# Products of ones placed on TensorE behind four norms' spreads and in the router

## The chip, the cores and the metric

The kernel runs on one core of a Trainium2 chip. The time is the device time of one execution in microseconds (us), taken as the median of several runs. One further execution is recorded by the hardware profiler, and all rows below are from it. [...]

## The reference, cut to what matters

The program computes two transformer blocks one after the other for 256 tokens of width 1024. The first has two layers, and in its layer 0 a context of 256 more tokens goes along. Each layer normalises, modulates, projects, mixes (attention and a long convolution), and then does the same with a gated feed-forward part:

```python
h = modulate(rms_norm(x, norm_mix[layer]), shift1, scale1)
q, k, v, hy, g = jnp.split(h @ w_in[layer], PROJ_SPLITS, axis=-1)
...
x = x + gate1 * x_mix
x = x + gate2 * swiglu(modulate(rms_norm(x, norm_ffn[layer]), shift2, scale2),
                       w_gate_up[layer], w_down[layer])
```

The second block has a mixer, a cross attention to a memory, and a mixture of 32 experts of which each token uses two. A router picks them: logits, a group, the two best experts of it, their gates, and the place of each token in its expert's list.

## The kernel before, in words

Activations lie with their features on the 128 partitions and tokens along the row: 512 columns (tokens and context) in layer 0, 256 in layer 1 and later. Weights come in units of 512 KB through a ring of six slots on SyncE's queue. ScalarE rounds a unit to its high part (`ac_split`, L434) and VectorE subtracts for the low part (`ve_split`, L442). Each product of a weight tile then is three matmuls, high by high, high by low and low by high (`pe_block`, L463; `pe_pair`, L478, does two blocks side by side, key by key).

A norm goes over all engines. ScalarE squares, VectorE adds the squares of tiles 0 to 6 (`ve_add_square`, L532), TensorE sums over the partitions with a column of ones (`pe_sum_seven`, L516, and `pe_sum_last`, L523), ScalarE takes the root (L559), VectorE the reciprocal (L570), and TensorE spreads the result to all partitions by `pe_spread` (L539): one product of 128 columns for each 128 tokens, in plain fp32. The trace shows each such fp32 product as two instructions, so a spread of four is a row of x8. Then the normalised tile k is made in a chain of four steps: VectorE multiplies by the root (L854), ScalarE scales and shifts (L835), GpSimd or ScalarE copies the high part (L847, L840), VectorE subtracts for the low part (L862). TensorE's next work, `pe_pair`, needs tile 0 to begin with (`pe.wait_ge(*ve_norm.at("low", ...))`) and a further tile after every six matmuls.

Four norms are followed by such a pair: "mix0" (before layer 0), "ffn0" (its feed-forward part, spread at the end of `pe_mix_out(0)`), "mix1" (at the end of `pe_down(0)`) and "ffn1" (at the end of `pe_mix_out(1)`). At "mix0" the spread comes early and two groups of modulation products (L601, L617) stand between it and the pair.

The order of the work on each engine is written out by hand in one program per engine (`tensor_program`, `scalar_program` and so on). PSUM banks are handed out in turn from a list: `banks.take` moves the first idle bank to the end of the list, and whoever takes a bank waits for its last reader.

In the router (`pe_router_steps`) TensorE transposes the logits and 16 tiles of the activations (`pe_to_rows`, L2262), then waits for VectorE's selection (`chosen`, L2337) and multiplies it by a triangle for the places (L2249 to L2254). The gather of the tokens (L2382) and the experts' products (L2433, L2477) follow. The experts' weights, 192 units of 1 MB, come on SyncE's queue (L2868) through 15 slots; the first 15 are queued behind the last weights of the cross attention, and every further one waits until its slot is spent.

Of the kernel before, what the change touches and what calls it, by code (L numbers as in the profile page):

```python
# [16 lines left out]
P = 128  # L17
# [253 lines left out]
def two_blocks_kernel(nc, T):  # L271
    ctx = ExitStack()
    with ctx:
        def sb(name, cols, dt=F32, rows=P):
            return ctx.enter_context(nc.sbuf_tensor(name, [rows, cols], dt))
# [31 lines left out]
        ones = sb("ones", P)  # L307
# [83 lines left out]
        banks = Slots([b[:, :] for b in psum])  # L391
# [143 lines left out]
        def pe_spread(pe, site, cols, give=True):  # L535
            pe.wait_ge(*landed["con"])
            pe.wait_ge(*ve_norm.at("rstd", site))
            for tb in range(cols // P):
                ins = pe.eng.matmul(banks.ap("sum", site)[:, tb * P:(tb + 1) * P],  # L539
                                    rsts.ap(site)[:, tb:tb + 1].to_broadcast([P, P]), ident, start=True, stop=True)  # L540
            ins.then_inc(*pe_sums.up("spread", site))
            if give:
                banks.give("sum", site)

        def ac_square(ac, site, n, chunk, cols):
            ac.wait_ge(*squares.emptied(site, n))
# [44 lines left out]
        def pe_mod_group(pe, g):  # L591
            if g == 0:
                banks.hold((ve_mod, ("added", 0, 0)), "mods")
            out = banks.take((ac_mod, ("rows", g)), "mod", g)
            pe.wait_ge(*banks.emptied("mod", g))
            pe.wait_ge(*ve_mod.at("silu", 1))
            for k in range(8):
                w, u = first.block("w_mod", 0, 32 * g + 4 * k, 4)
                pe.wait_ge(*first.arrived(u))
                c = k % 4  # L600
                ins = pe.eng.matmul(out[32 * c:32 * c + 32, :], sc2[:, k, :], w, start=k < 4, stop=k >= 4,  # L601
                                    tile_position=(0, 32 * c))
            ins.then_inc(*pe_mod.up("group", g))
            if g > 0:
                pe_mod_turn(pe, g - 1)
            if g == 3:
                pe_mod_turn(pe, g)
                banks.give("mods")
# [260 lines left out]
        def tokens(l):  # L869
            return 256 if l else 512  # L870
# [552 lines left out]
        def pe_mix_out(pe, l):  # L1423
            t, site = tokens(l), f"ffn{l}"

            def q_cut(k):
                pe.wait_ge(*ve_cut.at("q", l, k))

            pe_open(pe, site)
            pe_added(site)  # L1430
            for j in range(8):
                out = banks.take((ve_out, ("mix", l, j, t // 256 - 1)), "mix", l, j)
                pe.wait_ge(*banks.emptied("mix", l, j))
                pe_block(pe, ("mix", l, j), out[:, 0:t], "w_out", l, 8 * j, 8, lambda k: (hi_q(k, l), QL[:, k, 0:t]), q_cut)
            pe_sum_seven(pe, site, t)
            pe_sum_last(pe, site, t)
            pe_spread(pe, site, t)

        def ac_mix_out(ac, l):
            t, site = tokens(l), f"ffn{l}"  # L1440
# [137 lines left out]
        def pe_down(pe, l):  # L1578
            t, site = tokens(l), down_site(l)
            pe_added(site)  # L1580

            def three(half, k, n):
                m, b = 22 * half + k, 88 * half + 4 * k + n
                u, c = unit("w_down", l, b), (b % UB) * P
                hi, lo = cut_place(VTR, m, t), cut_place(YFR, m, t)
                pe.wait_ge(*ve_cut.at("ff", l, m))
                pe.wait_ge(*ve_lo.at(nth[u]))
                whi, wlo = hi_slot(nth[u])[:, c:c + P], lo_slot(u)[:, c:c + P]
                for i, (w, x) in enumerate(((whi, hi), (whi, lo), (wlo, hi))):
                    ins = pe.eng.matmul(banks.ap("ff", l, 4 * half + n)[:, 0:t], w, x, start=k == 0 and i == 0, stop=k == 21 and i == 2)  # L1590
                return ins, u

            for half in range(2):
                for n in range(4):
                    banks.hold((ve_out, ("ff", l, 4 * half + n, t // 256 - 1)), "ff", l, 4 * half + n)
                for n in range(4):
                    pe.wait_ge(*banks.emptied("ff", l, 4 * half + n))
                for k in range(19 if half else 22):
                    for n in range(4):
                        ins, u = three(half, k, n)  # L1600
                        if k == 21 and n < 3:
                            ins.then_inc(*pe_products.up("ff", l, half, n))
                    ins.then_inc(*pe_products.up("down", l, half, k))
                    stream.spent[u] = (pe_products, ("down", l, half, k))
                if half:
                    for n in range(4):
                        for k in range(19, 22):
                            ins, u = three(half, k, n)
                            stream.spent[u] = (pe_products, ("down", l, 1, 21))
                        ins.then_inc(*pe_products.up("ff", l, half, n) if n < 3 else pe_products.up("down", l, 1, 21))  # L1610
                for n in range(4):
                    banks.give("ff", l, 4 * half + n)
            if l == 0:
                pe_open(pe, site)
                pe_sum_seven(pe, site, t)
                pe_sum_last(pe, site, t)
                pe_spread(pe, site, t)


        def ac_down_squares(ac, l, j):  # L1620
# [615 lines left out]
        def pe_router_steps(pe):  # L2236
            out = banks.take((ve_router, ("logits", 1)), "by_token")
            pe.wait_ge(*banks.emptied("by_token"))
            pe.wait_ge(*ac_router.at("logits"))
            for tb in range(2):  # L2240
                ins = pe.eng.transpose(out[:, 36 * tb:36 * tb + 36], LT[:, tb * P:(tb + 1) * P], ident[0:36, 0:36])
            ins.then_inc(*pe_router.up("by_token"))
            pe_to_rows(pe, 0)
            pe_to_rows(pe, 1)
            out = banks.take((ve_router, ("place",)), "place")
            pe.wait_ge(*banks.emptied("place"))
            pe.wait_ge(*ve_router.at("chosen"))
            tri, both = LATE[:, 2, :], MM.rearrange("p b e -> p (b e)")
            pe.eng.matmul(out[:, 0:64], tri, both, start=True, stop=False)  # L2249
            pe.eng.matmul(out[:, 32:64], ones[:, :], MM[:, 0, :], start=False, stop=True).then_inc(*pe_router.up("place"))  # L2250
            out = banks.take((ve_router, ("most",)), "total")
            pe.wait_ge(*banks.emptied("total"))
            pe.eng.matmul(out[:, 0:32], ones[:, :], MM[:, 0, :], start=True, stop=False)
            pe.eng.matmul(out[:, 0:32], ones[:, :], MM[:, 1, :], start=False, stop=True).then_inc(*pe_router.up("total"))  # L2254

        def pe_to_rows(pe, tb):
            for half in range(2):
                out = banks.take((ac_router, ("rows", tb, half)), "rows2", tb, half)
                pe.wait_ge(*banks.emptied("rows2", tb, half))
                for k in range(4):  # L2260
                    pe.wait_ge(*ac_router.at("gain", 4 * half + k))
                    ins = pe.eng.transpose(out[:, k * P:(k + 1) * P], H2[:, 4 * half + k, tb * P:(tb + 1) * P], ident)  # L2262
                ins.then_inc(*pe_router.up("rows", tb, half))
# [444 lines left out]
        def tensor_program(pe):  # L2708
            pe_mod_group(pe, 0)
            pe_mod_group(pe, 1)  # L2710
            pe_open(pe, "mix0")
            pe_added("mix0")
            pe.wait_ge(*gp_start.at("ones"))
            pe_sum_seven(pe, "mix0", 512)
            pe_sum_last(pe, "mix0", 512)
            pe_spread(pe, "mix0", 512)
            pe_mod_group(pe, 2)
            pe_mod_group(pe, 3)
            for l in range(2):
                pe_heads(pe, l)  # L2720
                pe_hyena(pe, l)
                for n, a in enumerate(attention(l)):
                    pe_attend(pe, a, no_side if n else convolving(l, pe_conv_step))
                pe_merge(pe, l)
                pe_mix_out(pe, l)
                pe_gate_up(pe, l)
                pe_down(pe, l)
            pe_keys(pe)
            pe_mixer(pe)
            pe_mixed(pe)  # L2730
            pe_memory(pe)
            pe_router_steps(pe)
            pe_moe(pe)
            pe_output(pe)
# [274 lines left out]
```

## Time and profile before

| | |
|---|---|
| median of 3 runs | 2119.44 us (2115.68 to 2121.33) |
| profiled execution | 2115.06 us, of which the span of the instructions is 2113.3 us |
| TensorE busy | 1905.0 us (90%), 14008 matmuls |
| VectorE, ScalarE busy | 1133.7 us (54%), 891.7 us (42%) |
| granted TensorE clock, mean | 0.957 |
| DMA | 427.99 MB, mean 203 GB/s |

"Span" is the time from the first to the last instruction; the profiled execution's own time is 1.8 us longer. A busy time is the sum of the intervals in which an engine worked. In rows of the timeline the last bracket is the time for which the engine idled before that instruction, and who ended it. Matmuls are pipelined: a row's second number for x16 is from the start of the first to the end of the last, and the step from one to the next is shorter than one's own duration.

### The profile page before, as it was taken

How to read it: one execution, taken by the hardware profiler on the slowest of the kernel's cores; microseconds unless marked ns; L12 is line 12 of the kernel's file. 1: busy time of each engine (PE TensorE's matmuls, PEld its weight loads, DVE VectorE, ACT ScalarE, POOL GpSimd, SP SyncE). 2: the span in 40 equal slices, each digit the busy share in tenths (PEclk: the TensorE clock that was granted, in tenths of full speed). 3: DMA queues.
4: the chain of work that ended last, by engine and by line, in shares of the span. 5: the costliest groups of instructions: out<-in, count | busy, mean ns of one | idle time of the engine just before them, and what ended most of it. 6: DMA issues, size and time to landing. Idle time of an engine off the chain costs nothing.

```text
span 2113.3 us, 33439 instructions
## 1 busy us (share of the span) xinstructions
PE 1905.0 (90%) x14008; PEld 1544.2 (73%) x14008; DVE 1133.7 (54%) x1862; ACT 891.7 (42%) x1514; POOL 16.9 (1%) x31
## 2 busy tenths in 40 slices
PE   7999989999999999999899999999999777677766
PEld 3877667777777888788699999997898544455434
DVE  3454756666787788557655667779765111111011
ACT  4333445554766667444444555744845100000001
POOL 0000000000000000000000000000000000000000
PEclk9999999999999999999999999999999988888897
DMA  7222014453555555224045455543247999999995
GB/s 311 87 70 80 1 61 148 150 189 109 181 179 180 190 192 174 100 80 160 1 159 194 160 184 185 189 161 119 80 160 290 419 420 420 419 419 420 420 420 217
DMA packets 91120, 427.99 MB, mean 203 GB/s; under 512 B 11089, under 2 KB 12754, under 8 KB 66002
## 3 DMA queue, kind: packets, MB, share of 16 engines
q1 hardware_dynamic: 78866, 382.51, 48.3%
q10 hardware_dynamic: 12096, 43.26, 6.1%
q8 instruction: 113, 1.85, 0.4%
q14 instruction: 45, 0.37, 0.0%
HBM read 424.68 MB, written 1.05 MB: 201 GB/s over the span
## 4 chain that ended last, share of the span: by engine, by line
PE 67%; DMA 19%; DVE 7%; ACT 4%; issue 2%; SPq 1%; POOL 0%; DVEq 0%; ACTq 0%; POOLq 0%
PE bank L463 43%; PE bank L1590 8%; DMA area<-in_w 7%; DMA his<-in_w 4%; DMA ring<-in_w 4%; DMA PPT<-in_w 2%; PE bank L478 2%; PE bank L2477 2%; PE bank L2433 2%; DVE st L1261 1%; PE bank L1189 1%; PE bank L2085 1%; ACT PPT L1206 1%; PE bank L928 1%; DVE ring_r L442 1%
## 5 line engine op out<-in xcount | busy, mean ns | idle before, releaser
L463 PE MATMUL bank<-HH_r,his_r 128*128 128x256 f32 (+1 forms) x1504 | 501.9, 334 | 1.3 <-DVE ring_r L442 1.2
L442 DVE TENSOR_TENSOR ring_r<-ring,his_r 128x1024 fp32r<-128x1024 f32 x306 | 373.7, 1223 | 223.3 <-ACT his_r L434 222.0
L463 PE MATMUL bank<-HH_r,ring_r 128*128 128x256 f32 (+1 forms) x1504 | 490.3, 326 | 0.0
L463 PE MATMUL bank<-H_r,his_r 128*128 128x256 f32 (+1 forms) x1440 | 472.3, 328 | 0.0
L434 ACT ACTIVATE his_r<-ring 128x1024 fp32r<-128x1024 f32 x306 | 322.6, 1056 | 321.5 <-PE bank L463 233.9
L463 PEld LDWEIGHTS bank<-HH_r,his_r 128*128 128x128 f32 x1504 | 282.4, 188 | 36.9 <-issue 10.0
L463 PEld LDWEIGHTS bank<-HH_r,ring_r 128*128 128x128 f32 x1504 | 282.1, 188 | 24.8
L463 PEld LDWEIGHTS bank<-H_r,his_r 128*128 128x128 f32 x1440 | 270.5, 188 | 28.7 <-issue 2.6
L2449 DVE TENSOR_TENSOR tmp<-tmp,bank 128x128 f32<-128x128 f32 x64 | 18.4, 288 | 384.4 <-ACT tmp L2442 264.2
L2433 PE MATMUL bank<-area,KF 128*32 128x128 f32 x1888 | 87.6, 311 | 39.9 <-DMA area<-in_w 36.8
L463 PE MATMUL bank<-area_r,his_r 128*128 128x256 f32 (+1 forms) x384 | 121.9, 317 | 0.0
L1590 PE MATMUL bank<-VT_r,ring_r 128*128 128x512 f32 (+1 forms) x352 | 118.6, 337 | 0.0
L1590 PE MATMUL bank<-YF_r,his_r 128*128 128x512 f32 (+1 forms) x352 | 118.1, 335 | 0.0
L1590 PE MATMUL bank<-VT_r,his_r 128*128 128x512 f32 (+1 forms) x352 | 117.5, 334 | 0.0
L2433 PEld LDWEIGHTS bank<-area,KF 128*32 128x32 f32 x1888 | 70.9, 125 | 54.0 <-DMA area<-in_w 46.8
L2488 ACT ACTIVATE H<-bank 128x512 f32<-128x512 f32 x16 | 9.6, 597 | 195.5 <-PE bank L2477 195.5
L703 ACT ACTIVATE rst<-rst 128x1024 f32<-128x1024 f32 x80 | 83.5, 1044 | 0.6 <-DVE rst L695 0.6
L2477 PE MATMUL bank<-area,tmp 128*32 128x512 f32 x256 | 60.7, 680 | 22.4 <-DMA area<-in_w 21.7
L463 PEld LDWEIGHTS bank<-area_r,his_r 128*128 128x128 f32 x384 | 72.1, 188 | 5.8 <-issue 0.2
L1590 PEld LDWEIGHTS bank<-YF_r,his_r 128*128 128x128 f32 x352 | 66.1, 188 | 7.7
L1590 PEld LDWEIGHTS bank<-VT_r,his_r 128*128 128x128 f32 x352 | 65.9, 187 | 7.6 <-DVE YF_r L1333 0.2
L1329 ACT ACTIVATE VT_r<-area 128x512 fp32r<-128x512 f32 (+1 forms) x96 | 50.0, 524 | 50.9 <-PE bank L1590 45.3
(408 smaller groups left out, 3327.3 us busy)
## 6 DMA issues: line engine op xcount, KB each, us to landing
area<-in_w SPq DMA_DIRECT2D x91, 1024.0 KB, 27.2
ring<-in_w_in SPq DMA_DIRECT2D x102, 512.0 KB, 3.5
ring<-in_w_gate_up SPq DMA_DIRECT2D x88, 512.0 KB, 3.6
ring<-in_w SPq DMA_DIRECT2D x36, 1024.0 KB, 27.2
HH<-in_w SPq DMA_DIRECT2D x26, 1024.0 KB, 26.9
ring<-in_w_down SPq DMA_DIRECT2D x44, 512.0 KB, 3.5
KX<-in_w_mod_rows ACTq DMA_DIRECT2D x28, 512.0 KB, 3.4
VX<-in_w_mod_rows ACTq DMA_DIRECT2D x28, 512.0 KB, 3.5
```

The costliest lines, as they stand in the source:

```text
L434: ac.eng.activation(hi_slot(n), stream.slot(u), ACT.Copy).then_inc(*ac_hi.up(n))
L442: ve.eng.tensor_tensor(lo_slot(u), stream.slot(u), hi_slot(n).bitcast(F32), ALU.subtract).then_inc(*ve_lo.up(n))
L463: ins = pe.eng.matmul(out, a, b, start=k == 0 and m == 0, stop=end)
L478: ins = pe.eng.matmul(out, a, b, start=k + m == 0, stop=k == 7 and m == 2)
L703: ac.eng.activation(prod, prod, ACT.Copy, accum_out=MODS[l][:, j, s:s + 1]).then_inc(*ac_mod.up("sum", n, s))
L928: ins = pe.eng.matmul(vb[tb // 2][:, o:o + 256], x[:, k, sl], w, start=k == 0 and n == 0 and o == 0, stop=k == 7 and n == 2 and o > 0)
L1189: ins = pe.eng.matmul(out[:, 0:256], vs(kc), c.pts[g % 2][:, kc * 256:(kc + 1) * 256], start=kc == 0, stop=kc == c.nk - 1)
L1206: ac.eng.activation(p[:, m * w:(m + 1) * w], src[:, m * w:(m + 1) * w], ACT.Exp, bias=st[:, so + m:so + m + 1], scale=c.rq(h, i + m) if c. ...
L1329: ac.eng.activation(hi, src, ACT.Copy).then_inc(*ac_cut.up(*key))
L1590: ins = pe.eng.matmul(banks.ap("ff", l, 4 * half + n)[:, 0:t], w, x, start=k == 0 and i == 0, stop=k == 21 and i == 2)
L2433: ins = pe.eng.matmul(out[32 * n:32 * n + 32, 0:P], HG[g % 2][:, k, 32 * j:32 * j + 32], w, start=k == 0, stop=k == 7, tile_position=(0, 3 ...
L2477: ins = pe.eng.matmul(out[32 * j:32 * j + 32, :], AT[j][:, 32 * k:32 * k + 32], w, start=k == 0, stop=k == 3, tile_position=(0, 32 * j))
```

## The change

A helper `pe_idle` is added. It takes a bank, waits until it is free and until `ones` is set (which was at the very start), and issues n products of `ones` (128x128) by `ones` into the bank's first 128 columns, each overwriting the last. Nothing reads the bank. It is called with n = 12 between the modulation products and the first pair, 14 behind the spread of ffn0, 14 behind that of mix1, 10 behind that of ffn1, and 9 in the router between the transposes and the places.

```diff
--- before.py
+++ after.py
@@ -542,6 +542,15 @@
             if give:
                 banks.give("sum", site)
 
+
+        def pe_idle(pe, site, n):
+            out = banks.take((pe_sums, ("idle", site)), "idle", site)
+            pe.wait_ge(*banks.emptied("idle", site))
+            pe.wait_ge(*gp_start.at("ones"))
+            for i in range(n):
+                ins = pe.eng.matmul(out[:, 0:P], ones[:, :], ones[:, :], start=True, stop=True)
+            ins.then_inc(*pe_sums.up("idle", site))
+
         def ac_square(ac, site, n, chunk, cols):
             ac.wait_ge(*squares.emptied(site, n))
             ac.eng.activation(squares.ap(site, n)[:, 0:cols], chunk, ACT.Square).then_inc(*ac_squares.up(site, n))
@@ -1435,6 +1444,7 @@
             pe_sum_seven(pe, site, t)
             pe_sum_last(pe, site, t)
             pe_spread(pe, site, t)
+            pe_idle(pe, site, 14 if l == 0 else 10)
 
         def ac_mix_out(ac, l):
             t, site = tokens(l), f"ffn{l}"
@@ -1615,6 +1625,7 @@
                 pe_sum_seven(pe, site, t)
                 pe_sum_last(pe, site, t)
                 pe_spread(pe, site, t)
+                pe_idle(pe, site, 14)
 
 
         def ac_down_squares(ac, l, j):
@@ -2242,6 +2253,7 @@
             ins.then_inc(*pe_router.up("by_token"))
             pe_to_rows(pe, 0)
             pe_to_rows(pe, 1)
+            pe_idle(pe, "place", 9)
             out = banks.take((ve_router, ("place",)), "place")
             pe.wait_ge(*banks.emptied("place"))
             pe.wait_ge(*ve_router.at("chosen"))
@@ -2716,6 +2728,7 @@
             pe_spread(pe, "mix0", 512)
             pe_mod_group(pe, 2)
             pe_mod_group(pe, 3)
+            pe_idle(pe, "mix0", 12)
             for l in range(2):
                 pe_heads(pe, l)
                 pe_hyena(pe, l)
```

## Rows read from the trace of the kernel before

**Rows 1.** The page: granted clock in 40 slices, and the chain's shares by engine.
```profile
PEclk9999999999999999999999999999999988888897
PE 67%; DMA 19%; DVE 7%; ACT 4%; issue 2%; SPq 1%; POOL 0%; DVEq 0%; ACTq 0%; POOLq 0%
```

**Rows 2.** The chain of waits in order: start, us, what; four pairs, two blocks, the gather.
```profile
39.16 11.94 PE bank L478 x45
...
66.22 5.51 PE bank L463 x24
...
516.07 13.04 PE bank L478 x48
...
903.32 13.23 PE bank L478 x45
...
931.68 2.82 PE bank L463 x24
...
1171.90 7.43 PE bank L478 x48
...
1630.78 6.35 PE bank L2382 x32
```

**Rows 3.** Timeline of TensorE ahead of the five places: start, us, what, idle before.
```profile
34.12 1.95 PE L617 MATMUL bank<-con,PPT 128*128 128x2 f32 x16
...
511.27 1.16 PE L539 MATMUL bank<-con,st 128*128 128x128 f32 x8 [0.57 <-DVE st L570]
...
898.17 1.51 PE L539 MATMUL bank<-con,st 128*128 128x128 f32 x8 [1.31 <-DVE st L570]
...
1168.24 1.02 PE L539 MATMUL bank<-con,st 128*128 128x128 f32 x4 [0.55 <-DVE st L570]
...
1624.74 1.97 PE L2262 MATMUL bank<-con,H 128*128 128x128 f32 x16
...
1628.88 0.43 PE L2249 MATMUL bank<-X 128*128 128x64 f32 x2 [2.17 <-DVE X L2337]
```

**Rows 4.** Windows: length, busy PE, PEld, DVE, ACT, POOL, then PEclk, DMA share, GB/s.
```profile
36.00:43.00 7.00, 3.91 (x12) 3.10 (x12) 3.20 (x7) 6.36 (x13) 2.69 (x4) 0.76 0.93 339
511.00:521.00 10.00, 6.08 (x22) 4.92 (x23) 7.94 (x14) 7.69 (x16) 3.09 (x4) 0.66 0.00 0
898.00:911.00 13.00, 9.19 (x30) 7.32 (x31) 9.61 (x18) 10.21 (x19) 4.55 (x6) 0.61 0.00 2
1168.00:1177.00 9.00, 6.12 (x34) 5.86 (x35) 6.67 (x18) 6.16 (x11) 3.01 (x6) 0.62 0.10 39
1629.00:1638.00 9.00, 8.69 (x76) 8.46 (x80) 4.77 (x18) 1.88 (x6) 0.00 (x0) 0.62 1.01 422
```

**Rows 5.** Windows of 1 us in which the clock fell, at four of the places.
```profile
38.00:39.00 1.00, 0.00 (x0) 0.00 (x0) 0.59 (x1) 1.00 (x3) 0.63 (x2) 0.83 1.03 410
...
513.00:514.00 1.00, 0.00 (x0) 0.00 (x0) 1.00 (x3) 0.75 (x2) 0.00 (x0) 0.56 0.00 0
...
898.00:899.00 1.00, 0.83 (x6) 0.83 (x7) 0.12 (x2) 0.00 (x0) 0.00 (x0) 0.91 0.06 21
...
1168.00:1169.00 1.00, 0.76 (x4) 0.73 (x4) 0.17 (x1) 0.00 (x0) 0.00 (x0) 0.74 0.83 340
```

**Rows 6.** A window of fp32 products of 128 columns at the low clock (L2382).
```profile
1631.00:1636.00 5.00, 5.00 (x24) 5.00 (x25) 3.62 (x12) 0.60 (x1) 0.00 (x0) 0.50 1.02 426
```

**Rows 7.** Timeline of VectorE: the first and the last of ffn0's eight low tiles.
```profile
515.12 0.69 DVE L862 TENSOR_TENSOR H_r<-H,HH_r 128x512 fp32r<-128x512 f32 x1 [0.78 <-POOL HH_r L847]
...
523.52 0.69 DVE L862 TENSOR_TENSOR H_r<-H,HH_r 128x512 fp32r<-128x512 f32 x1 [0.51 <-POOL HH_r L847]
```

**Rows 8.** A window of the router and the first experts.
```profile
1620.00:1640.00 20.00, 17.52 (x199) 16.03 (x201) 9.32 (x49) 8.34 (x16) 0.00 (x0) 0.83 1.01 422
```

**Rows 9.** Timeline of SyncE's queue: the first experts' unit, and the sixteenth.
```profile
1601.32 0.43 SPq L2868 DMA_DIRECT2D con<-in_w  x1
...
1639.07 0.33 SPq L2868 DMA_DIRECT2D con<-in_w  x1
```

## The prediction

> **What bounds the kernel now.** I read the page first. Its chain of waits gives TensorE 67% of the span, DMA 19%, VectorE 7% [rows 1]: up to the router TensorE decides, and the DMA share is all in the experts at the end. So a microsecond won on TensorE before about 1600 us should come off the whole. The clock line stands at 9 or less nearly everywhere, which hides short falls, so I went on to the chain in order of time. At four places a pair of blocks (L478) follows a norm. A block of 24 matmuls at full clock takes 5.51 us with 512 columns and 2.82 us with 256, steps of 0.230 and 0.118 [rows 2]. By these the pairs should take 10.3 us (45 matmuls, mix0 and mix1), 11.0 (48, ffn0) and 5.6 (48, ffn1). They took 11.94, 13.23, 13.04 and 7.43: too much by 1.6, 2.9, 2.0 and 1.8. About 0.2 of each is the filling of the pipeline after a wait and stays; the rest is the clock: 1.4, 2.7, 1.8 and 1.6, together 7.5 us.
>
> The windows say when it was low. A mean clock c over a length L means 2(1-c)L at the low level: 3.4 us at mix0, 6.8 at ffn0, 10.1 at mix1, 6.8 at ffn1 and 6.8 in the router [rows 4]. The fall is dated by windows of 1 us [rows 5]: 38.7, 513.1, 898.8 and 1168.5. Each follows a stretch in which TensorE idled or did one-column sums and little else; the clock came back only after the pair had kept the engine full for a while. The idle times that are to be filled: mix0 from 36.07 (34.12 + 1.95) to 39.16, 3.1 us; ffn0 from 512.4 to 516.07, 3.6; mix1 from 899.7 to 903.32, 3.6; ffn1 from 1169.3 to 1171.90, 2.6; the router 2.2 [rows 2, 3].
>
> **The change part by part.** Nothing is removed. Added are 12, 14, 14, 10 and 9 fp32 products of 128 columns. The trace shows one as two instructions (a spread of four is x8), so 24, 28, 28, 20 and 18 instructions, 118 in all. What one takes: at full clock 8 of them stand in 1.16 us and 16 in 1.97 [rows 3], so the step lies between 0.10 (8 more in 0.81) and 0.12 (1.97/16), and I take 0.113; at the low clock 24 in 5.00 us, 0.208 [rows 6]. So the four fillings and the router's take 2.7, 3.2, 3.2, 2.3 and 2.0 us at full clock, all inside their idle times, and 5.0, 5.8, 5.8, 4.2 and 3.7 at the low one, all longer than them. What is queued behind them on TensorE is the pair itself, so every microsecond beyond the idle time delays it.
>
> [...]
>
> mix0: the filling starts at 36.07 with the clock high and ends at 38.8, before the pair's 39.16 and about when the clock fell with nothing there. TensorE is then hardly idle at all, so I take the fall as gone: gain 1.4.
>
> ffn0: TensorE has done little since the sums, and the fall at 513.1 comes 0.9 us after the filling can start (512.2, the spread's start and eight steps). Bounds: if the fall goes, 1.8. If it comes all the same, 8 instructions are done at full clock, and with the shortest low stretch seen, 3.4 us, 16 more at the low one; the last 4 take 0.5, and the pair starts at 517.0, 0.9 late but at full clock: gain 0.9.
>
> mix1: the fall at 898.8 is ahead of the filling, in the middle of the spread, so the filling can't prevent it, only end it sooner. From 899.3 (six of the spread's steps are high, two low) with a low stretch of 3.4 us (to 902.2) 14 are done low, the other 14 take 1.6, and the pair starts at 903.8, 0.5 late: gain 2.2. With a low stretch of 6.8 us all 28 are low, the pair starts 1.8 late with 0.5 us of low clock left: gain about 0.6. With no fall, 2.7.
>
> ffn1: the fall at 1168.5 is again inside the spread. From 1168.9 to 1171.9 14 are done low, the other 6 take 0.7, the pair starts at 1172.5, 0.6 late: gain 1.0; with no fall 1.6.
>
> The sum is 5.5 us with the falls where they were and 7.5 with none. When the clock falls is not fixed to the program: the same idle pattern gave low stretches of 3.4, 6.8 and 10.1 us [rows 4], and after mix0's gain all later places lie earlier. I take 6.2, nearer the low end, because two of the four falls, mix1's and ffn1's, come before their filling begins, and nothing new stands ahead of them.
>
> What could eat it. The pair at full clock needs a low tile every 6 x 0.230 = 1.38 us; VectorE's eight of ffn0 start between 515.12 and 523.52, one per 1.20 us [rows 7], so they keep ahead. The helper's waits are for a bank that was freed long before and for `ones` from the start: 0. One more turn of the bank list moves each later user by one bank, and the oldest in the list is always several uses old: 0. No DMA, ScalarE or VectorE instruction is added or moved.
>
> Router: 18 instructions take 2.0 us from about 1626.7 and end just ahead of L2249's 1628.88 [rows 3]. If they keep the clock high, the gather's 32 take 3.6 us in place of 6.35 [rows 2], and with the places before it some 3.0 us are won there. I put them at 0. From 1601.3 on 15 units of 1.05 MB lie in SyncE's queue, and the sixteenth is issued at 1639.07 [rows 9]; at 422 GB/s 15 units take 37 us, and the DMA engines are full throughout [rows 8]. An earlier first expert frees its slot into a queue that isn't empty, and from there on DMA paces the end. The cover is thin: 37 us of transfers against 37.8 between the two issues. In an execution in which TensorE is a microsecond later there, DMA would run dry and the router's gain would count. The bounds are 0 and 3.0.
>
> Forecast: 6.2 us. The profiled execution would go from 2115.1 to 2108.9. The median of the runs is 4.4 us above it, and the forecast is for the median: 2119.4 - 6.2 = 2113.2.
>
> **The rivals.** First, the router counts too, and the falls go nearly everywhere: 7.5 + 3.0 = 10.5 us, 2108.9. For it speaks the thin cover; against it a DMA share of 1.01 in the very window in which the clock was low. Second, nothing is left: the clock stays low for as long as before, or what the pairs gain is lost in overruns and in waits behind them (the unit splits of L434 and L442 run one or two units ahead). That gives 2119, within 2 either way. For it speaks that two of the four falls lie ahead of the filling. Against it: at all four places the clock rose once TensorE was kept full, and the fillings keep it full some 3 us sooner. Third, on the other side: products of ones run at the low clock and don't bring it back. Then they overrun at 0.208 each: mix0 36.1 + 5.0 = 41.1, 1.9 late; ffn0 2.0; mix1 1.8; ffn1 1.2, and the pairs lose what they lose now. That is 6.9 us more, 2126.3. It decides from where the clock is low at the start of a filling and the filling doesn't count as work; for it speaks that mix1's and ffn1's start low, against it that at mix0 the clock was still high when TensorE had been idle for 2.6 us.
>
> **How the numbers follow.** The forecast has 0.62, the first rival 0.18, no gain 0.14, the third 0.06. A measurement of this kernel tells about 0.3% from no change, 6.4 us, and the forecast lies right at that bound: of its cases a little under half are beyond it. So faster 0.46 (0.28 + 0.18), same 0.49, slower 0.05. The range is 2107.5 to 2119.5: from the first rival's full gain with a little on top to no gain. The forecast's own range is 2111 to 2115.
>
> **What would show it.** In the changed kernel's windows mix0 should have a clock of 1.00 from 36 to 43 and its pair take 10.5 us for 45 matmuls in the chain. ffn0, mix1 and ffn1 should show pairs of 11.2, 10.5 and 5.8 us that start up to 1 us later behind their spreads than now, with no idle time ahead where the clock was low. The router's gather should be 3.6 us and the experts' DMA share still 1.01 with the last landings earlier only by what was won before it. It is wrong if the pairs still begin at the low clock, if a filling's instruction takes other than 0.11 or 0.21, or if the span shrinks by less than the pairs and their starts gain, which would put a wait behind them.

## The result and the profile after

| | before | after |
|---|---|---|
| median | 2114.92 us (2112.81 to 2121.33, 9 runs) | 2109.05 us (2106.04 to 2110.17, 9 runs) |
| ratio | | 0.9964, interval 0.9954 to 0.9973 |
| profiled execution | 2115.06 us, span 2113.3 | 2106.04 us, span 2104.2 |
| granted clock, mean | 0.957 | 0.966 |

The changed kernel is faster by 0.36%, 7.6 us of 2117 (5.7 to 9.7 by the interval); the ratio is taken with more runs of the kernel before than the nine of the table. Its profiled execution is the lowest of its nine.

The page after: TensorE's busy time and count, the clock in 40 slices, the chain by engine. TensorE has 118 matmuls more, as the prediction counted, and its share of the chain falls from 67% to 64% [rows 1].

```profile
PE 1906.4 (91%) x14126; PEld 1549.9 (74%) x14126; DVE 1133.6 (54%) x1862; ACT 891.9 (42%) x1514; POOL 17.0 (1%) x31
...
PEclk8999999999999999999999999999999988988898
...
PE 64%; DMA 20%; DVE 8%; ACT 5%; issue 2%; SPq 2%; ACTq 0%; POOL 0%; DVEq 0%; POOLq 0%
```

The chain of waits after, as in [rows 2]: start, us, what. The rows of 45 matmuls take 10.3 to 10.6 us where they took 11.94 to 13.23 (ffn0's before, 13.04, counts 48), the 48 of ffn1 5.89 for 7.43, the gather 3.81 for 6.35. The fillings (L551) of ffn0 and mix1 have become links of the chain: there the pair waits for them.

```profile
39.24 10.60 PE bank L478 x45
...
512.86 4.09 PE bank L551 x28
516.95 10.32 PE bank L478 x45
...
899.23 3.78 PE bank L551 x28
903.00 10.43 PE bank L478 x45
...
1168.47 5.89 PE bank L478 x48
...
1625.54 3.81 PE bank L2394 x32
...
2086.03 3.62 PE bank L2489 x26
```

TensorE's timeline after, as in [rows 3]: at mix0, ffn1 and in the router the filling ends 0.15 to 0.41 us before the work behind it can begin; at ffn0 the pair follows without a gap.

```profile
36.02 2.92 PE L551 MATMUL bank<-ones 128*128 128x128 f32 x24
39.24 0.50 PE L478 MATMUL bank<-HH_r,his_r 128*128 128x512 f32 x1 [0.30 <-DVE H_r L871]
...
512.65 4.30 PE L551 MATMUL bank<-ones 128*128 128x128 f32 x28
516.71 0.48 PE L478 MATMUL bank<-HH_r,his_r 128*128 128x512 f32 x1
...
1165.66 2.40 PE L551 MATMUL bank<-ones 128*128 128x128 f32 x20
1168.47 0.35 PE L478 MATMUL bank<-HH_r,his_r 128*128 128x256 f32 x1 [0.41 <-DVE H_r L871]
...
1621.41 2.17 PE L551 MATMUL bank<-ones 128*128 128x128 f32 x18
1623.74 0.43 PE L2261 MATMUL bank<-X 128*128 128x64 f32 x2 [0.15 <-DVE X L2349]
```

The granted clock is a share of full speed, and these profiles show two levels of it, here called high and low. Of the first 2090 windows of 1 us 1893 are at 1.00 and 135 at 0.50 before, 1924 and 106 after; the other 62 and 60 lie between, where it changes. The windows of [rows 4] after, in the same columns: the clock is 1.00, 0.83, 0.91, 1.00 and 1.00 where it was 0.76, 0.66, 0.61, 0.62 and 0.62.

```profile
36.00:43.00 7.00, 6.70 (x42) 5.86 (x42) 3.21 (x7) 6.27 (x13) 2.61 (x4) 1.00 0.91 340
511.00:521.00 10.00, 9.96 (x55) 9.21 (x56) 7.33 (x13) 7.25 (x15) 3.09 (x4) 0.83 0.00 0
898.00:911.00 13.00, 13.00 (x70) 11.52 (x70) 9.95 (x18) 10.22 (x19) 4.54 (x6) 0.91 0.01 1
1168.00:1177.00 9.00, 8.56 (x71) 8.36 (x71) 6.97 (x16) 7.44 (x12) 2.22 (x4) 1.00 0.21 68
1629.00:1638.00 9.00, 7.80 (x253) 7.05 (x255) 1.36 (x6) 2.82 (x5) 0.00 (x0) 1.00 1.01 420
```

The two that aren't 1.00, in windows of 1 us: at ffn0 the clock is at 0.50 through the filling's first half and back before its end; at mix1 the fall is over by 901. So there the filling did not prevent the fall; the low stretch was spent on products that nobody needs, and the pair began at full clock.

```profile
511.00:512.00 1.00, 0.96 (x5) 0.96 (x6) 0.00 (x0) 0.00 (x0) 0.00 (x0) 0.67 0.00 0
512.00:513.00 1.00, 1.00 (x7) 1.00 (x6) 0.10 (x1) 0.00 (x0) 0.00 (x0) 0.50 0.00 0
...
514.00:515.00 1.00, 1.00 (x7) 1.00 (x7) 0.78 (x2) 1.00 (x3) 0.09 (x1) 0.62 0.00 0
515.00:516.00 1.00, 1.00 (x11) 1.00 (x10) 0.44 (x1) 1.00 (x3) 0.71 (x2) 1.00 0.00 0
...
900.00:901.00 1.00, 1.00 (x9) 1.00 (x8) 1.00 (x2) 0.95 (x2) 0.00 (x0) 0.77 0.00 0
```

**Where the 9.1 us between the two profiles lie.** A span falls into three parts: up to the issue of the experts' first unit on SyncE's queue, from there to the first product behind the last landing (the transfers), and the rest behind it. SyncE's timeline after has the issue at 1596.83, before at 1601.32 [rows 9].

```profile
1596.83 0.43 SPq L2881 DMA_DIRECT2D con<-in_w  x1
```

The last landing's products start at 2086.03 after and at 2090.87 before. So: 4.5 us were won before the issue, 0.35 in the transfers, and 4.2 behind the last landing (18.2 us for 22.4). The last is not the change's, as the further profiles of both kernels show (18.2 us in a second one of before, 19.9 in a second one of after). In the chain of before its first row stands for 26 matmuls that took 6.60 us, with a granted clock of 0.57 from 2090 to 2098; after they took 3.62 at 1.00:

```profile
2090.87 6.60 PE bank L2477 x26
2097.47 3.65 PE bank L2500 x16
```

In all eleven experiments that part took between 18.1 and 22.4 us, in kernels with fillings and without. The first 4.5 us are less than the four places gave. From the start of the spread to the start of the pair's last matmul, by the timelines:

| place | before | after | gain | forecast |
|---|---|---|---|---|
| mix0 (from the last modulation products, 34.12 and 34.21) | 17.26 | 15.91 | 1.35 | 1.4 |
| ffn0 | 17.45 | 16.51 | 0.94 | 0.9 to 1.8 |
| mix1 | 18.66 | 16.57 | 2.09 | 2.2 |
| ffn1 | 10.81 | 8.97 | 1.84 | 1.0 to 1.6 |

They give 6.22 us. Some of it was lost again at places that the change does not touch. The clearest is the first scores of layer 1's attention; first the chain of before, then of after. The scores begin 1.84 us earlier after and end only 0.89 earlier, because TensorE's two products take 2.06 us in place of 1.11. The clock in the window from 994 to 1002 is 1.00 before and 0.79 after.

```profile
998.22 1.11 PE bank L1162 x2
```

```profile
996.38 2.06 PE bank L1171 x2
```

The same happens in layer 0 (1.43 us before, 2.06 after), where 0.6 us is lost. Such a fall is not fixed to the program: in a second profile of the changed kernel both took 1.11 us, and in a second one of the kernel before layer 0's took 2.06.

### The profile page after: what moved, and what is told of

It reads as the page before. It is cut to its first block, busy times and chain, and to the rows that moved or that the text cites. A ratio compares the mean times of both kernels' runs of the same rounds, so it can differ in the third digit from the quotient of the medians.

```text
span 2104.2 us, 33676 instructions
## 1 busy us (share of the span) xinstructions
PE 1906.4 (91%) x14126; PEld 1549.9 (74%) x14126; DVE 1133.6 (54%) x1862; ACT 891.9 (42%) x1514; POOL 17.0 (1%) x31
## 4 chain that ended last, share of the span: by engine, by line
PE 64%; DMA 20%; DVE 8%; ACT 5%; issue 2%; SPq 2%; ACTq 0%; POOL 0%; DVEq 0%; POOLq 0%
PE bank L463 41%; PE bank L1600 8%; DMA area<-in_w 5%; DMA HH<-in_w 4%; DMA ring<-in_w 4%; DMA con<-in_w 3%; PE bank L2445 2%; PE bank L478 2%; DVE st L1270 1%; DMA his<-in_w 1%; DMA PPT<-in_w 1%; PE bank L1198 1%; PE bank L2096 1%; SPq L2881 1%; PE bank L937 1%
## 5 line engine op out<-in xcount | busy, mean ns | idle before, releaser
L442 DVE TENSOR_TENSOR ring_r<-ring,his_r 128x1024 fp32r<-128x1024 f32 x306 | 373.6, 1223 | 215.8 <-ACT his_r L434 214.3
```

What stands on the lines that cost most here:

```text
L442: ve.eng.tensor_tensor(lo_slot(u), stream.slot(u), hi_slot(n).bitcast(F32), ALU.subtract).then_inc(*ve_lo.up(n))
```

## The experiments

All ratios are against the kernel before on the same chip. "Issue", "transfers" and "end" are the three parts of the profiled span as above.

| kernel | median, us | ratio (interval) | issue | transfers | end |
|---|---|---|---|---|---|
| before | 2114.92 | | 1601.3 | 489.6 | 22.4 |
| before again | 2114.22 (1 run) | | 1605.1 | 489.1 | 18.2 |
| one column, once | 2117.48 | 1.0002 (0.9993 to 1.0010) | 1601.4 | 489.4 | 19.8 |
| router alone | 2116.49 | 0.9999 (0.9987 to 1.0011) | 1606.3 | 489.0 | 20.2 |
| after | 2109.05 | 0.9964 (0.9954 to 0.9973) | 1596.8 | 489.2 | 18.2 |
| after again | 2109.81 | 0.9972 (0.9962 to 0.9982) | 1598.4 | 489.0 | 19.9 |
| four norms alone | 2111.10 | 0.9970 (0.9960 to 0.9980) | 1598.0 | 488.9 | 22.4 |
| last landing too | 2109.83 | 0.9965 (0.9953 to 0.9977) | 1598.5 | 491.0 | 18.6 |
| sums too | 2108.50 | 0.9957 (0.9942 to 0.9972) | 1598.6 | 489.4 | 18.1 |
| attention too | 2110.26 | 0.9964 (0.9951 to 0.9976) | 1599.7 | 489.9 | 19.8 |
| one column wide | 2121.19 | 1.0025 (1.0015 to 1.0034) | 1607.0 | 489.3 | 18.2 |
| doubled | 2118.61 | 1.0011 (1.0001 to 1.0021) | 1604.2 | 489.3 | 18.1 |
| all together | 2104.69 | 0.9951 (0.9939 to 0.9963) | 1595.1 | 489.2 | 18.7 |

**Which of the five counts: four norms alone, router alone.** The first leaves out one call, the second the other four.

```diff
             pe_to_rows(pe, 1)
-            pe_idle(pe, "place", 9)
```

> The changed kernel without the router's filling: only the four norms have theirs. Theory (the router is hidden by the experts' transfers): the gather takes about 6.3 us again in place of 3.8, the second con unit is issued some 3 us later, and the time is that of the changed kernel, about 7.5 us under the kernel before (ratio 0.9964). Rival (the thin cover is gone in most executions): 3 us of the gain are lost, ratio about 0.998.

Measured: 0.9970, interval 0.9960 to 0.9980. The gain is there without the router's filling. That the ratio is 0.0006 above the changed kernel's can't be told from nothing. The gather took 3.81 us in its profile though nothing was placed ahead of it: there the clock was high anyway (1.00 from 1628 to 1631).

```diff
-            pe_idle(pe, site, 14 if l == 0 else 10)
...
-                pe_idle(pe, site, 14)
...
-            pe_idle(pe, "mix0", 12)
```

> The kernel before with the router's filling alone. Theory: the gather falls to about 3.8 us, the last landing doesn't move, ratio 1.000 within 0.001. Rival: 3 us come off, ratio 0.9985; and if what the changed kernel won behind the last landing (4.2 us in its profile) hangs on the router's filling and not on chance, ratio 0.998.

Measured: 0.9999, interval 0.9987 to 1.0011. The gather took 3.81 us, as in every profile with the router's filling (one column wide and doubled too), and the filling is worth nothing in the time. Without it the gather took 6.35, 5.44 and (with a single product there) 5.17 us, but also 3.81 in the experiment above, so the profiles alone don't prove that the filling shortened it. From the issue to the products behind the last landing it is 488.9 to 489.9 us in every kernel but the one with fillings at that landing, whatever the gather takes.

**Is it the work, or the banks and waits? One column, once.** All five calls stay with their bank turns and waits, but each issues one product of one column.

```diff
-            for i in range(n):
-                ins = pe.eng.matmul(out[:, 0:P], ones[:, :], ones[:, :], start=True, stop=True)
+            for i in range(1):
+                ins = pe.eng.matmul(out[:, 0:1], ones[:, :], ones[:, 0:1], start=True, stop=True)
```

> All five calls stay with their bank turn, waits and signal, but each issues one product of one column in place of 9 to 14 of 128. Theory (the gain is the clock, through TensorE's work): low stretches as before, pairs of 11.9, 13.0, 13.2 and 7.4 us within the spread of where the clock falls, ratio 1.000 within 0.001. Rival (the order of the PSUM banks or the shift of the later code is part of the gain): the span shrinks by up to 4.5 us without any pair getting shorter, ratio 0.998.

Measured: 1.0002, interval 0.9993 to 1.0010, and pairs of 11.95, 11.95, 12.57 and 7.46 us, low as before. The calls, the waits and the shift of the banks cost nothing and give nothing that can be told.

**How much must stand there: one column wide, doubled.** The first keeps the counts and takes one column of `ones`; the second has twice as many products.

```diff
-                ins = pe.eng.matmul(out[:, 0:P], ones[:, :], ones[:, :], start=True, stop=True)
+                ins = pe.eng.matmul(out[:, 0:1], ones[:, :], ones[:, 0:1], start=True, stop=True)
```

> The changed kernel's five fillings with the same number of products, each with one column in place of 128. They take TensorE as long (its one-column sums take 0.12 us per instruction, as the wide ones 0.11), but almost nothing streams through the array. Theory (the clock goes by what is streamed, not by the time that instructions stand on the engine): low stretches and pairs as in the kernel before, ratio 1.000 within 0.0015. Rival (an instruction on the engine is enough): as the changed kernel, 0.9965.

Measured: 1.0025, interval 1.0015 to 1.0034, slower by 5.3 us, which neither the theory nor the rival had. Its chain:

```profile
36.10 4.36 PE bank L551 x24
40.46 11.96 PE bank L478 x45
...
515.40 5.76 PE bank L551 x28
```

A narrow product stood there as long as a wide one at the low clock (5.76 / 28 = 0.206 us, against 0.208 in [rows 6]), so the fillings overran; and the pairs behind them still began low. All four pairs begin at 0.50 (12.24, 12.06 and 7.07 us behind mix0's). Windows of 1 us at mix0: TensorE is busy all the time, and the clock falls all the same and stays down for the rest of the filling and the start of the pair.

```profile
36.00:37.00 1.00, 1.00 (x10) 1.00 (x10) 0.44 (x3) 0.35 (x1) 0.00 (x0) 0.90 0.99 398
37.00:38.00 1.00, 1.00 (x7) 1.00 (x6) 0.00 (x0) 1.00 (x3) 0.20 (x1) 0.50 1.03 414
...
42.00:43.00 1.00, 1.00 (x3) 0.74 (x3) 0.69 (x1) 1.00 (x3) 0.63 (x2) 0.50 0.18 40
```

This comes near the prediction's third rival: 5.3 us where it had worked out 6.9. With 128 columns the same stretch of the changed kernel was granted 1.00 in its first profile. But not in its second, where the fall came within the filling as here (chain, then windows):

```profile
35.92 4.41 PE bank L551 x24
40.34 10.34 PE bank L478 x45
```

```profile
36.00:37.00 1.00, 1.00 (x6) 1.00 (x6) 0.40 (x3) 0.53 (x2) 0.00 (x0) 0.50 1.02 411
...
38.00:39.00 1.00, 1.00 (x7) 1.00 (x6) 0.69 (x1) 1.00 (x4) 0.63 (x2) 0.50 1.01 406
39.00:40.00 1.00, 1.00 (x9) 1.00 (x9) 0.54 (x1) 0.97 (x3) 0.43 (x1) 0.83 1.05 423
```

So a filling of full width did not always keep the clock up either. What the two differ in is the way back: with 128 columns the low stretch ended before the pair (3.4 us by the windows), with one column it lasted 6.8 us, through the filling and some 3 us into the pair.

```diff
-            for i in range(n):
+            for i in range(2 * n):
```

> Twice as many products at each of the five places (24, 28, 28, 20, 18). Theory (what doesn't fit into the idle time is paid in full at 0.226 us a product): 59 products more are 13.3 us, of which about 1 us fits into what idle time is left and the router's 2 us are hidden, so some 10 us more than the changed kernel up to the first experts' transfer, ratio to before 1.001. Rival (a part of them is hidden since VectorE's low tiles or the unit splits were the bound after the pair): 5 us or less, ratio 0.999.

Measured: 1.0011, interval 1.0001 to 1.0021, 0.0047 or 10 us above the changed kernel. The pairs are at the high clock in all four places (10.3 us, and 5.45 at ffn1), but start at 41.72, 520.89, 910.17 and 1177.52:

```profile
36.25 5.46 PE bank L551 x48
41.72 10.34 PE bank L478 x45
```

The 50 products more at the norms are 11.3 us at 0.226, so nearly all that is beyond the idle time is paid. Counts between these two, or below the change's, were not run.

**More places: sums, attention, last landing.** A few products between the squares' sums and the spread, where the clock falls at mix1 and, in the changed kernel, at ffn0:

```diff
             pe_sum_seven(pe, site, t)
+            pe_idle(pe, site + "a", 3 if l == 0 else 1)
             pe_sum_last(pe, site, t)
+            pe_idle(pe, site + "b", 2)
...
+                pe_idle(pe, site + "a", 1)
                 pe_sum_last(pe, site, t)
+                pe_idle(pe, site + "b", 5)
```

> The changed kernel, and short fillings also ahead of the fillings: between the sum of seven squares and the last one (3, 1, 1 products at ffn0, mix1, ffn1) and between that and the spread (2, 5, 2). Theory (at ffn0, mix1 and ffn1 the clock falls in the sparse stretch of the sums, before the long filling begins, and about 0.9, 0.7 and 0.6 us are lost by the filling's overrun at the low clock): no low clock between the sums and the pair, the fillings take 3.2, 3.2 and 2.3 us and end inside the idle time, 1.5 to 2.5 us less up to the first experts' transfer, ratio to before 0.9955. Rival (what was lost was lost to the phase of the clock alone): as the changed kernel, 0.9965.

Measured: 0.9957, interval 0.9942 to 0.9972. In its profile the falls at ffn0 and mix1 are gone: the filling of mix1 stands in 3.29 us and the pair waits 0.52 for VectorE again and not for the filling.

```profile
902.18 3.29 PE L551 MATMUL bank<-ones 128*128 128x128 f32 x28
905.99 0.47 PE L478 MATMUL bank<-HH_r,his_r 128*128 128x512 f32 x1 [0.52 <-DVE H_r L871]
```

But its issue is at 1598.6, no earlier than the changed kernel's, and the ratios can't be told apart: inconclusive. The four places took 56.2 us together, for 58.0 after; further on TensorE waited 2.44 us for a weight unit of ffn0, a wait that the next section comes to.

```diff
+                pe_idle(pe, f"att{l}", 8 if l else 12)
```

stands ahead of each layer's attention.

> The changed kernel, and a filling ahead of the first scores of the attention in both layers (12 products at layer 0, idle 3.4 us; 8 at layer 1, idle 2.2 us). Theory (part of the gain at mix0 and mix1 was given back there by a fall that the kernel before did not have at that place, 0.6 and 0.9 us in the profiles): no fall between the last projection and the first table load, up to 1.5 us less up to the first experts' transfer, ratio about 0.996. Rival (the falls there come as often in the kernel before and cost nothing on average, because softmax on ScalarE and VectorE sets the pace): no difference, 0.9965.

Measured: 0.9964, interval 0.9951 to 0.9976. The first scores took 1.11 us in both layers, but so they did in the changed kernel's second profile and in the one with fillings at the last landing, without any filling there. So nothing shows that this filling did it, and the time shows no difference: the rival stands.

Five products ahead of each of the last four waits for a unit of the experts' weights (the bank and its signal are left out here):

```diff
+                            if g == 7 and u == 1 and half == 0 and k == 2:
+                                for n in range(5):
+                                    ins = pe.eng.matmul(spare[:, 0:P], ones[:, :], ones[:, :], start=True, stop=True)
```

> The changed kernel, and five products of ones (1.1 us at full clock) ahead of each of the last four waits for a unit of the experts' last weights, where TensorE idled 1.2 to 1.4 us of each 2.5. Theory (what lies behind the last landing runs at whatever level the clock happens to have, 22.4 us in the profile of before and 18.2 in that of after): it is 18.2 or a little less in every execution, and the median is 1 to 3 us under the changed kernel's, ratio to before about 0.9955. Rival (the tail's level isn't chance but already mended by the change): no difference from the changed kernel, 0.9964.

Measured: 0.9965, interval 0.9953 to 0.9977. The end behind the last landing took 18.6 us, near its lowest, but the fillings themselves now reached past the landing (the transfers' part is 491.0 and not 489), which its chain shows with one of them ahead of the last products:

```profile
2088.24 1.31 PE bank L2492 x10
2089.55 3.55 PE bank L2497 x26
```

So what could be won there went into the overrun in part, 1 to 2 us by these two numbers. The edit can't be told from the changed kernel.

**All three together**, with three products for five at the last landing.

> All fillings at once: the changed kernel's, those beside the sums of the norms, those ahead of the attention's first scores, and three products (not five) ahead of each of the last four waits for the experts' weights. Theory (each keeps the clock at the high level where it stands and costs nothing inside idle time): up to the first experts' transfer 1 to 3 us less than the changed kernel, behind the last landing 18.2 us in each execution, the median 3 to 4 us under the changed kernel's and a smaller spread, ratio to before 0.995. Rival (the softmax and the transfers cover them): as the changed kernel, 0.9965.

Measured: 2104.69 us (2104.16 to 2109.76, 6 runs), 0.9951, interval 0.9939 to 0.9963: 5.1 us under the changed kernel on the same chip (2109.81, 2107.12 to 2113.52 in 9 runs). By the median it is the fastest of all; the two ranges and the two intervals overlap a little, so the size of the step is loose. Its windows at the four norms:

```profile
36.00:43.00 7.00, 6.70 (x41) 5.84 (x42) 3.21 (x7) 6.45 (x13) 2.78 (x4) 1.00 0.91 336
511.00:521.00 10.00, 9.48 (x58) 8.24 (x57) 8.57 (x14) 8.88 (x18) 3.60 (x5) 1.00 0.01 2
896.00:909.00 13.00, 12.45 (x72) 10.84 (x73) 9.98 (x18) 10.22 (x19) 4.53 (x6) 1.00 0.01 2
1163.00:1172.00 9.00, 8.57 (x72) 8.23 (x71) 7.26 (x15) 7.41 (x12) 2.55 (x5) 1.00 0.15 56
```

The clock is 1.00 in all of them, and the issue is at 1595.1, the earliest seen. None of the three parts could be told from nothing alone.

**The two kernels of the case again**, beside it.

> The changed kernel as it is, on the same chip as the one with all fillings, for a direct comparison and a second profile of it. Theory (the place of the clock's falls outside the filled places is chance): first experts' transfer between 1596 and 1600, the part behind the last landing anywhere between 18.1 and 22.4 us, ratio 0.9965. Rival (the 4.2 us behind the last landing belong to the change): 18.2 again.

Measured: 0.9972, interval 0.9962 to 0.9982, and an end of 19.9 us, not the 18.2 of the first profile: that end does not belong to the change. The pairs start at full clock at mix0, ffn0 and mix1, and at ffn1 the clock is 0.92 in the microsecond from 1169. At ffn1 the filling took 3.82 us on the chain, with a fall within it, where the first profile had none (2.40).

> The kernel before as it is, for a second profile. Theory: low stretches at the four pairs of 3 to 10 us again but at other moments; first experts' transfer between 1600 and 1607; behind the last landing anything from 18.1 to 22.4 us. Rival (its tail is always slow): 22.4 again.

Measured: issue at 1605.1, pairs of 13.32, 12.39, 12.50 and 8.21 us, end 18.2. The kernel before can have a fast end too.

## Why the prediction was right and wrong

**The mechanism was right in the main.** The pairs start at the high clock behind fillings of full width, and the gain is there with the norms' fillings and not with the router's, nor with one product of one column. ffn0: the fall came all the same, and already within the spread (0.67 in the microsecond from 511, where [rows 5] has it at 513.1); the pair started at 516.95 on the chain (forecast 517.0), at full clock. mix1: the low stretch was a short one, the pair started at 903.00. Steps of 0.113 and 0.208 us per instruction stand (24 in 2.92 us and 20 in 2.40 at full clock, 0.12 each with the last one's end; 28 narrow ones in 5.76 us at the low clock). The low stretches come out by windows of 1 us as 2(1-c)L has them: before, mix1's is 0.50 in each of the ten from 899 to 909, with 0.91 ahead and 0.97 behind, 10.2 us for 10.1. The 0.2 us that stay after a wait, for which no row stood, are there: the changed kernel's pair of mix0, at 1.00 throughout, took 10.60 us, 0.25 more than 45 steps of 0.230; its first product took 0.50 us and the second began 0.34 after it, and the further ones stand 0.39 each at a step of 0.23.

One step of it does not hold in every execution: "TensorE is then hardly idle at all, so I take the fall as gone" at mix0. It was gone in the first profile (1.00 from 36 to 43), but in the second the clock fell at 36.0 with TensorE busy in every microsecond, and the pair started at 40.34, about a microsecond late.

**The router at nothing was right**: 0.9999 with its filling alone. 3 us would be 0.9985, just outside the interval of 0.9987 to 1.0011, and the first rival falls with it. The thin cover held in every profile: some 489 us from wherever the first issue is.

**The bank turns at nothing were right**: 1.0002.

**The step that failed is the size of the sum**, and with it the outcome that was put first. I forecast 6.2 us of gain, at the bound of 6.4, and gave "no difference that can be told" 0.49 and faster 0.46. Measured are 7.6 us (5.7 to 9.7), faster and clear of no change. The sum was worked out from one profile, and the four places vary between profiles. Four kernels have no filling of full width at the norms (before, before again, router alone, one column once), and four have the change's (after, after again, four norms alone, last landing too). From the start of the spread to the start of the pair's last matmul, means of four profiles each:

| place | without | with | gain | forecast |
|---|---|---|---|---|
| mix0 | 17.89 | 16.18 | 1.7 | 1.4 |
| ffn0 | 17.90 | 16.55 | 1.4 | 0.9 to 1.8 |
| mix1 | 18.64 | 16.55 | 2.1 | 2.2 |
| ffn1 | 10.94 | 9.40 | 1.5 | 1.0 to 1.6 |
| all | 65.4 | 58.7 | 6.7 | 6.2 |

- ffn1 was taken at 1.0, with the fall inside the spread. In two of the four it was so (9.94 and 9.95), in the other two there was no fall (8.97 and 8.76).
- The stock of which the gains were parts, "together 7.5 us", was that of a cheap profile. In the same way (the pairs' sum, ffn0's taken for 45, less 36.5 at full clock and 0.8 that stays) the four without lose 7.6 (before), 9.1 (before again), 9.5 (router alone) and 6.6 us (one column, once), mean 8.2.

**"What could eat it: 0" was wrong as well**, in the other direction. The issue of the experts' first unit is at 1601.3, 1605.1, 1606.3 and 1601.4 without, mean 1603.5, and at 1596.8, 1598.4, 1598.0 and 1598.5 with, mean 1597.9: 5.6 us reach it of the 6.7. Most of what is missing in these means is a wait that grew. Some 60 us into ffn0 TensorE takes up a weight unit whose low part VectorE makes (L442). In three of the four profiles with the fillings it waited 2.73, 2.44 and 2.63 us there (after again, four norms alone, last landing too), and 0.17 in the first; without them 0, 1.04, 0 and 0.36. From the last matmul of ffn0's pair to mix1's spread it is 371.4 us with and 369.8 without, on average. In the second profile of the changed kernel the chain goes there through a load of modulation rows (first row) to that wait (second, of the timeline):

```profile
562.08 5.63 DMA VX<-in_w_mod_rows
```

```profile
576.59 0.47 PE L463 MATMUL bank<-HH_r,his_r 128*128 128x512 f32 x1 [2.73 <-DVE ring_r L442]
```

The sum's paragraph had compared the pair with VectorE's low tiles only; the waits for the unit splits stand in the second rival, and there as a reason for no gain at all. In the first pair of profiles this wait was small, and what ate 1.7 of 6.2 us were in part falls of the clock at waits that were there before (the first scores of both layers, 0.6 and 0.9 us). So my 6.2 came out near the 5.6 of the issues with one error for each sign. That the medians show 7.6 and not 5.6 is not explained by the profiles.

**The base of the forecast** was further off than its gain: 2119.44 was the median of 3 runs, and nine have 2114.92. The 2113.2 forecast is 4.2 us too high, of which some 2.7 are that (2109.05 / 0.9964 = 2116.7) and 1.4 the gain.

**The rivals.** No gain falls: the interval of the ratio ends at 0.9973, and that of its repetition at 0.9982. The third does not hold for this kernel; the kernel with one column wide comes near it.

**What stays open.** How the 7.6 us divide over the four places: the intervals are about 2 us either way, and I have not switched them one by one. Why 5.6 us by the profiles' issues are 7.6 in the first comparison and 5.9 in its repetition (0.9972): the latter's interval, 3.8 to 8.0 us, holds 5.6, and the former's begins at 5.7. Whether the wait in ffn0 grew because TensorE came earlier or because the load of rows happened to be slower: in the three kernels with more fillings it was 2.44 (sums too), 0 (attention too) and 0.91 us (all together), and no run holds that load fixed. What decides whether the end behind the last landing has the low clock: it happened in kernels of both kinds. And which of the three added parts gives the best kernel its last 5 us, or whether its shorter wait in ffn0 (0.91 us) has a share in them.

## What to carry to other kernels

Where TensorE waits some 3 us for a chain on other engines and then has a long run of products ahead, unread products of 128 columns in the wait let that run begin at the high clock in nearly every profile here (in one, ffn1's began at 0.54): worth 1.4 to 2.1 us for each place in the mean of four profiles. Size them by the idle time at full clock (twice as many cost 10 us). One column wide they cost 5.3 us. Placed ahead of the short sums too they took away the falls there in two profiles, but alone that was not to be told in the time. Ahead of work that a queue of transfers covers they were worth nothing here (the router's alone: 0.9999). Ask what TensorE will meet when it comes earlier, here a weight unit not yet split, and read several profiles before pricing a clock, since one execution's falls are a sample.

## What was not expected of the hardware

- A plain fp32 product of one column stood as long as one of 128 columns at the low clock, 0.206 us per instruction for 0.208. Ahead of mix0's pair TensorE was busy with them in every microsecond and was granted 0.50 from 37 to 43. With 128 columns it was granted 1.00 there in one profile; in another it fell at 36.0 and was back in the microsecond from 39.
- The same 26 products behind the last landing took 6.60 us in one execution and 3.62 in another of the same kernel. This end alone moves a span by 4.2 us, as much as the whole gain up to the experts in the case's two profiles.
